# A mixture-of-experts decoder layer: moving the gather of each expert pair's rows, and the sums of the down biases, to other places in TensorE's order

## The chip, the core and the metric

The kernel runs on one core of a Trainium2 chip. The core has a matrix engine (TensorE, PE in the profile), a vector engine (VectorE, DVE), a scalar engine (ScalarE, ACT), GpSimd (POOL) and a queue that mostly issues transfers (SyncE, SP). The engines run side by side and wait for each other through semaphores. Each engine takes its own instructions in the order in which they are written. The metric is the device time of one execution in microseconds (us).

## The reference

The program computes one layer of a decoder for 288 tokens (256 of a prompt, 32 new ones of eight sequences): attention in two head groups, an output projection, a LayerNorm, and then a mixture of experts (MoE) with 32 experts, of which each token uses four. All numbers are float32. The change lies in the MoE, which is most of the time:

```python
def moe_ffn(hx, w_router, b_router, w_gate_up, b_gate_up, w_down, b_down):
    logits = jnp.matmul(hx, w_router).astype(jnp.float32) + b_router
    top_val, top_idx = lax.top_k(logits, TOP_K)                 # 4 of 32
    gates = jax.nn.softmax(top_val, axis=-1)
    comb = jnp.sum(jax.nn.one_hot(top_idx, N_EXPERTS) * gates[..., None], axis=1)

    def expert_step(acc, xs):
        wgu, bgu, wdn, bdn, c = xs                              # 1024x2048, 2048, 1024x1024, 1024
        gu = jnp.matmul(hx, wgu) + bgu
        gate = jnp.minimum(gu[:, 0::2], SWIGLU_LIMIT)
        up = jnp.clip(gu[:, 1::2], -SWIGLU_LIMIT, SWIGLU_LIMIT)
        act = gate * jax.nn.sigmoid(SWIGLU_ALPHA * gate) * (up + 1.0)
        y = jnp.matmul(act, wdn) + bdn
        return acc + c[:, None] * y.astype(jnp.float32), None
```

After it come a residual sum and a LayerNorm. The weights of the 32 experts are 403 MB, and every expert's weights are read once.

## The kernel before

The experts are taken in 16 pairs. A pair computes both experts side by side, each in one half (64 columns) of the matrix array, for at most 64 token rows ("slots") per expert. Further passes for experts with more rows are not taken in the profiled execution.

**Weights.** A pair's weights are 12 units of 2 MB: units 0 to 7 belong to the gate/up product, 8 to 11 to the down product. They go through a ring of 9 slots. SyncE issues each unit's transfer (`load_whole`, L508) as soon as its slot is free. For that it waits on counters that TensorE raises: `unit_used` after every second gate/up unit and after the second down unit, `gate_up_done` after unit 7, `down_done` after unit 11.

**One pair on TensorE** is, in this order:

- `begin_gate_up(i)` (L1267): the gate/up biases go into the four sum banks 0 to 3;
- `gate_up(i)` (L1171): units 0 to 7, each against a 128-row piece of the pair's turned rows `xg`. Behind unit 3 stands `combine(i - 1)` (L1251, L1237): the preceding pair's results are spread back to the tokens, five products that VectorE adds to `acc` (L2080);
- `gather(i + 1)` (L1051, L1055): the rows of the next pair are picked out of `hx` by products with a 0/1 matrix `pick`, into banks 6 and 7. ScalarE copies them to `xtok`, which is the same memory as `ybuf` (L1417);
- `turn_weights(i)` (L732 on `pickw`): the combining weights are transposed;
- `turn_act(i)` (L732 on `up`): the activations are transposed, in two halves of four; the first half waits for VectorE's products of the first two banks (`act_ready`), the second for those of the last two. ScalarE copies each half to `actT`;
- `down(i)` (L1224): units 8 to 11. Behind units 8 and 9 stand the transposes of the next pair's gathered rows (`turn_slots(i + 1)`, L732 on `ybuf`), which ScalarE scales into `xg` (L1562).

**VectorE** runs `swiglu(i)` when the four banks of gate/up are done: for each bank a minimum (L2062), a clip (L2063), a product (L2066), and, after ScalarE's sigmoid (L1571), the last product (L2071). It also makes the next `pick` matrix (`pick_slots`, L2046).

**The down biases** of all experts are summed once for all tokens, as products of the combining weights with the bias table (`add_biases`, L1122, and `add_sample_biases`, L1129). In the kernel before this stands between the down units of pair 12 (`finish_with_biases(MIDDLE, ...)`, with `MIDDLE = 12`).

`finish(i)` is the piece of TensorE's order that runs from the end of `gate_up(i)` to the end of `gate_up(i + 1)`. Nothing schedules these instructions: the order is the one written.

Of the kernel before, what the change touches and what calls it, by code (L numbers as in the profile page):

```python
# [26 lines left out]
PAIRS = E // 2  # L27
# [82 lines left out]
def build_layer(nc, x_prompt, x_sample, cache_k, cache_v, state_k, state_v, page_table, w_in, gn_moba,  # L110
# [222 lines left out]
    PERIOD = 3  # L333
# [3 lines left out]
    def slot_of(r, u):  # L337
        return (UNITS * r + u - 1) % RING
# [5 lines left out]
    def pass_slot(u):  # L344
        return u % 8

    def pass_value(i, u):

        if 4 <= u < 8:
            return i * 16 + (16 - 16 * PAIRS)  # L350
        return i * 32 + (16 * (u // 8 + 1) - 32 * PAIRS)
# [3 lines left out]
    def start_slot(u):  # L355

        return u if u < ASIDE else u - 1
# [5 lines left out]
    ln_bs = place("ln_bs", [128, 256], at=last_at + 9216)  # L363

    EARLY, WHOLE, LATE = range(3)
    MIDDLE = 12
    WHOLES = range(1, PAIRS - 1)
    USED_LATE = -2 * len(WHOLES)
    COPIES = 16 * (2 * DB + 5 + DB)
# [360 lines left out]
    def _(pe):  # L730
# [317 lines left out]
        def gather_samples():  # L1048
            for a in range(2):
                r = slice(NS * a, NS * a + NS)  # L1050
                nc.tensor.matmul(bank[6 + a][:, :], pick[r, 2, :], hx[r, 2, 512 * a:512 * a + 512], start=True, stop=False,  # L1051
                                 tile_position=(NS * a, 0))

        def gather_tile(t, a):
            return nc.tensor.matmul(bank[6 + a][:, :], pick[:, t, :], hx[:, t, 512 * a:512 * a + 512], start=False,  # L1055
                                    stop=(t == 1))
# [76 lines left out]
        def gather(i, turned_before):  # L1133
            pe.wait_ge(S.picked, i * 2 + 1)
            pe.wait_ge(S.actT_ready, turned_before)
            gather_samples()
            for a in range(2):
                gather_tile(0, a)
                gather_tile(1, a).then_inc(S.gathered, 1)
# [8 lines left out]
        def gate_up(i, m, odd, between={}, whole=False, further=False):  # L1148
            early = isinstance(i, int) and i == 0
            if not early:  # L1150
                begin_gate_up(i)
            for k in range(KC):
                w = [ring[slot_of(odd, k)][:, 2048 * e:2048 * e + 2048] for e in range(2)]
                if early:
                    pe.wait_ge(*((S.xg_ready, k // 4 + 1) if k % 4 == 3 else (S.first_slots, 3 * (k // 4) + k % 4 + 1)))
                if early:
                    w = [first[e] if k == ASIDE else ring[start_slot(k)][:, 2048 * e:2048 * e + 2048] for e in range(2)]
                    pe.wait_ge(*((S.first_in, 48) if k == ASIDE else (unit_in[start_slot(k)], 16)))
                elif further:
                    w = [ring[pass_slot(k)][:, 2048 * e:2048 * e + 2048] for e in range(2)]  # L1160
                    pe.wait_ge(half_in[pass_slot(k)], pass_value(i, k))
                elif whole:
                    w = [ring[slot_of(odd, k - k % 2 + e)][:, 2048 * (k % 2):2048 * (k % 2) + 2048] for e in range(2)]
                    if k % 2 == 0:
                        for u in (k, k + 1):
                            pe.wait_ge(unit_in[slot_of(odd, u)], unit_value(m, odd, u))
                else:
                    pe.wait_ge(unit_in[slot_of(odd, k)], unit_value(m, odd, k))
                for n in range(4):
                    for e in range(2):  # L1170
                        ins = nc.tensor.matmul(bank[n][64 * e:64 * e + 64, :], xg[:, k, 64 * e:64 * e + 64],  # L1171
                                               w[e][:, 512 * n:512 * n + 512], start=False, stop=(k == KC - 1))
                    if k == KC - 1:
                        ins.then_inc(S.gate_up_done, 1)
                if whole and k % 2 and k < KC - 1:
                    ins.then_inc(S.unit_used, 2)
                if not whole and k < KC - 1:
                    ins.then_inc(S.unit_used, 1)
                if k in between:
                    between[k]()  # L1180
# [61 lines left out]
        def combine(i):  # L1242
            pe.wait_ge(S.y_ready, i * 2 + 2)
            pe.wait_ge(S.spread_ready, i + 1)
            for j in range(5):
                t, half = divmod(j, 2)
                t0, rows = TILES[t]
                if j >= 2:
                    pe.wait_ge(S.added, i * 5 + (5 + j - 1))
                if t < 2:  # L1250
                    ins = nc.tensor.matmul(bank[4 + half][:, :], spread[:, t0:t0 + rows],  # L1251
                                           ybuf[:, 512 * half:512 * half + 512], start=True, stop=True)
                else:
                    ins = mix_samples(bank[4], True)
                ins.then_inc(S.mixed, 1)
# [14 lines left out]

        def finish(i, m, odd, m_next, whole=True, next_whole=True):

            gather(i + 1, i * 2)
            turn_weights(i, i * 2 + 3)
            turn_act(i, i * 2 + 4)
            down(i, m, odd, {0: lambda: turn_slots(i + 1, 0),
                             1: lambda: (pe.wait_ge(S.actT_ready, i * 2 + 2), turn_slots(i + 1, 1))}, whole)
            if m_next is not None:
                gate_up(i + 1, m_next, (odd + 1) % PERIOD, {3: lambda: combine(i)}, next_whole)

        def finish_with_biases(i, m, odd, m_next):

            def first_slots():
                turn_slots(i + 1, 0)
                turn_comb()

            def other_slots():
                pe.wait_ge(S.actT_ready, i * 2 + 2)
                turn_slots(i + 1, 1)
                for j in range(2):  # L1290
                    add_biases(j)

            def other_biases():
                for j in range(2, 4):
                    add_biases(j)
                add_sample_biases()

            gather(i + 1, i * 2)
            turn_weights(i, i * 2 + 3)
            turn_act(i, i * 2 + 4)  # L1300
            down(i, m, odd, {0: first_slots, 1: other_slots, 2: other_biases}, True)
            pe.wait_ge(S.bias_added, 5)
            gate_up(i + 1, m_next, (odd + 1) % PERIOD, {3: lambda: combine(i)}, True)

        begin_gate_up(0)
        logits_product(2)
# [3 lines left out]
        gate_up(0, 0, 0)  # L1310
        finish(0, 0, 0, 0, whole=False)
        finish(1, 0, 1, 0)
        finish(2, 0, 2, 1)

        def finish_three(m):
            finish(m * PERIOD, m, 0, m)
            finish(m * PERIOD + 1, m, 1, m)
            finish(m * PERIOD + 2, m, 2, m + 1)

        with pe.Fori(1, MIDDLE // PERIOD) as m:  # L1320
            finish_three(m)
        finish_with_biases(MIDDLE, MIDDLE // PERIOD, 0, MIDDLE // PERIOD)
        finish(MIDDLE + 1, MIDDLE // PERIOD, 1, MIDDLE // PERIOD)
        last = PAIRS - 1
        finish(last - 1, last // PERIOD - 1, 2, None)

        def keep_sums(t, half, stop=False):

# [83 lines left out]
    def _(act):  # L1412
# [138 lines left out]
        def take_gathered(i):  # L1551
            for a in range(2):
                act.wait_ge(S.gathered, i * 2 + (a + 1))
                copy(xtok[:, 512 * a:512 * a + 512], bank[6 + a][:, :]).then_inc(S.xtok_ready, 1)
# [13 lines left out]
        def sigmoids(i, ns=range(4)):  # L1568
            for n in ns:
                act.wait_ge(S.clipped, i * 4 + (n + 1))  # L1570
                nc.scalar.activation(sig[:, half_of(n)], gate[:, half_of(n)], ACT.Sigmoid, scale=SWISH).then_inc(S.sigmoided, 1)  # L1571
# [11 lines left out]
        def take_down(i):  # L1583
            act.wait_ge(S.down_done, i + 1)
            for half in range(2):
                copy(ybuf[:, 512 * half:512 * half + 512], bank[4 + half][:, :]).then_inc(S.y_ready, 1)

        take_gathered(0)
        take_slots(0)
        sigmoids(0)  # L1590

        def between_pairs(i):
            take_gathered(i + 1)
            take_weights(i)
            take_turned(i)
            take_slots(i + 1)
            take_down(i)

        def between_with_biases(i):
            take_gathered(i + 1)  # L1600
            take_weights(i)
            take_turned(i)
            act.wait_ge(S.comb_turned, 1)
            copy(combT[0:E, :], bank[3][0:E, 0:T]).then_inc(S.combT_ready, 1)
            take_slots(i + 1)
            take_down(i)

        with act.Fori(0, MIDDLE) as i:
            between_pairs(i)
            sigmoids(i + 1)  # L1610
        between_with_biases(MIDDLE)
        sigmoids(MIDDLE + 1)
        with act.Fori(MIDDLE + 1, PAIRS - 2) as i:
            between_pairs(i)
            sigmoids(i + 1)
        between_pairs(PAIRS - 2)
        sigmoids(PAIRS - 1, (0, 1))
        take_weights(PAIRS - 1)
        take_turned(PAIRS - 1, (0,))
# [607 lines left out]
```

## Time and profile before

| | us |
|---|---|
| median of 3 runs | 1141.97 |
| the 3 runs | 1142.9, 1140.39, 1141.97 |
| the profiled execution | 1139.37 |
| its span, first to last instruction | 1137.5 |
| PE busy in the span | 1099.5 |
| DVE busy | 293.1 |
| ACT busy | 203.6 |
| POOL busy | 30.0 |

The page divides the span into 40 slices of 28.4 us. The first 7 or so are the attention; the MoE fills the rest. The median lies 2.6 us above the profiled execution, 1.9 us of whose own time lie outside the span. In the views below, a time at a row's start is counted from the span's start; L with a number is a line of the kernel; `x16` is a count of instructions. A float32 product is two instructions in these records, so one unit is 16 of them.

### The profile page before, as it was taken

Reading aid. Unit: us, or ns where it says so; the run is one execution under the profiler, and the core shown is the slowest. Engines: PE = TensorE matmul, PEld = TensorE weight load, DVE = VectorE, ACT = ScalarE, POOL = GpSimd, SP = SyncE. Lnnn points to the kernel's source line nnn. Section 1 sums busy time; section 2 is a strip of 40 time slices with the busy share of each in tenths; the row PEclk is TensorE's granted clock in tenths of the full one; section 3 lists DMA queues with packets and bytes.
Section 4 is the critical chain, followed back from the end, with each engine's and each line's share of the span. In section 5 each row is a group of like instructions: output and inputs, shape, how many; then the busy total and the mean of one; then the engine's idle time right before and its main releaser. Section 6 shows DMA issues by size and latency. Waiting matters only on the chain.

```text
span 1137.5 us, 14116 instructions
## 1 busy us (share of the span) xinstructions
PE 1099.5 (97%) x5468; PEld 463.2 (41%) x5469; DVE 293.1 (26%) x734; ACT 203.6 (18%) x481; POOL 30.0 (3%) x65
## 2 busy tenths in 40 slices
PE   8999999999999999999999999999999999999996
PEld 6876764433333333333333333333333333333331
DVE  1553757530303030212121212120203031303033
ACT  2323412411111120202020202020201111111102
POOL 0110111000000000000000000000000000000001
PEclk9999999999999999999999999999999999999998
DMA  9967878999999999999999999999999999999994
GB/s 361 351 219 248 285 280 336 426 433 407 430 421 430 430 431 430 431 430 429 432 431 432 432 430 432 432 432 429 433 430 432 432 430 432 431 430 430 425 426 160
DMA packets 59172, 454.37 MB, mean 399 GB/s; under 512 B 6467, under 2 KB 19411, under 8 KB 31348
## 3 DMA queue, kind: packets, MB, share of 16 engines
q1 hardware_dynamic: 56642, 440.97, 92.7%
q0 software_dynamic: 1728, 10.75, 2.5%
q10 hardware_dynamic: 754, 1.98, 0.4%
q8 instruction: 34, 0.56, 0.2%
q14 instruction: 14, 0.11, 0.0%
HBM read 450.14 MB, written 11.93 MB: 406 GB/s over the span
## 4 chain that ended last, share of the span: by engine, by line
PE 83%; DMA 13%; ACT 2%; DVE 2%; issue 1%; SPq 0%; DVEq 0%
PE bank L1171 30%; PE bank L1224 19%; DMA ring<-in_w_gate_up 13%; PE bank L732 6%; PE bank L759 6%; PE bank L1055 5%; PE bank L1251 3%; PE bank L762 2%; PE bank L920 2%; PE bank L1051 1%; PE bank L1354 1%; PE bank L1267 1%; PE bank L877 1%; ACT ybuf L1417 1%; ACT actT L1417 1%; PE bank L851 1%
## 5 line engine op out<-in xcount | busy, mean ns | idle before, releaser
L1171 PE MATMUL bank<-ring,xg 128*64 128x512 f32 x2032 | 445.6, 594 | 10.8 <-DMA ring<-in_w_gate_up 10.8
L1171 PEld LDWEIGHTS bank<-ring,xg 128*64 128x64 f32 x2032 | 146.4, 137 | 299.3 <-issue 296.9
L1224 PE MATMUL bank<-ring,actT 128*64 128x512 f32 x960 | 216.2, 597 | 4.2 <-ACT actT L1417 4.2
L2080 DVE TENSOR_TENSOR acc<-acc,bank 128x512 f32<-128x512 f32 x60 | 41.3, 688 | 492.0 <-PE bank L1251 491.8
L1571 ACT ACTIVATE sig<-gate 128x256 f32<-128x256 f32 x64 | 26.5, 416 | 530.1 <-DVE gate L2062 530.1
L1224 PEld LDWEIGHTS bank<-ring,actT 128*64 128x64 f32 x960 | 67.3, 137 | 120.0 <-issue 115.3
L2062 DVE TENSOR_SCALAR gate<-bank 128x256 f32<-128x256 f32 x64 | 26.8, 419 | 186.8 <-PE bank L1171 186.8
L759 PE MATMUL bank<-xT,wblk 128*128 128x288 f32 x256 | 65.4, 409 | 0.3 <-DVE xT L1670 0.3
L1562 ACT ACTIVATE xg<-bank,small 128x128 f32<-128x128 f32 x128 | 48.0, 457 | 97.0 <-PE bank L732 96.9
L1055 PE MATMUL bank<-hx,pick 128*128 128x512 f32 x128 | 59.2, 605 | 0.0
L1417 ACT ACTIVATE ybuf<-bank 128x512 f32<-128x512 f32 x63 | 36.0, 596 | 126.7 <-PE bank L1224 87.4
L1251 PE MATMUL bank<-ybuf,spread 128*128 128x512 f32 x120 | 58.4, 619 | 0.0
L759 PEld LDWEIGHTS bank<-xT,wblk 128*128 128x128 f32 x256 | 47.5, 190 | 14.6 <-issue 2.7
L1055 PEld LDWEIGHTS bank<-hx,pick 128*128 128x128 f32 x128 | 23.0, 190 | 34.3 <-issue 34.3
L1251 PEld LDWEIGHTS bank<-ybuf,spread 128*128 128x128 f32 x120 | 19.2, 189 | 39.0 <-DVE acc L2080 19.7
L920 PE MATMUL bank<-wout,outT 128*128 128x512 f32 x64 | 29.8, 603 | 0.0
L762 PE MATMUL bank<-wblk,xT 128*128 128x256 f32 x128 | 29.0, 380 | 0.0
L2066 DVE SCALAR_TENSOR_TENSOR up<-up,gate 128x256 f32<-128x256 f32 x64 | 27.2, 425 | 3.3
L732 PEld LDWEIGHTS bank<-keep,ybuf 128*128 128x128 f32 x128 | 17.8, 207 | 25.3 <-issue 24.3
L723 POOL TENSOR_TENSOR acc<-acc,ln_b_sb 128x512 f32<-128x512 f32 x2 | 3.0, 1500 | 941.0 <-DVE acc L2186 941.0
L2063 DVE TENSOR_SCALAR up<-bank 128x256 f32<-128x256 f32 x64 | 26.5, 414 | 0.0
L2071 DVE TENSOR_TENSOR up<-up,sig 128x256 f32<-128x256 f32 x64 | 25.4, 419 | 0.0
(247 smaller groups left out, 672.3 us busy)
## 6 DMA issues: line engine op xcount, KB each, us to landing
ring<-in_w_gate_up SPq DMA_DIRECT2D x127, 2048.0 KB, 26.5
ring<-in_w_down SPq DMA_DIRECT2D x63, 2048.0 KB, 28.0
wblk<-in_w_in SPq DMA_DIRECT2D x11, 1024.0 KB, 8.7
kring<-in_cache_k_moba SPq DMA_DIRECT2D x16, 256.0 KB, 7.5
vring<-in_cache_v_moba SPq DMA_DIRECT2D x16, 256.0 KB, 7.2
out<-in_state_k_win POOLq DMA_DIRECT2D x8, 512.0 KB, 5.2
out<-in_state_v_win POOLq DMA_DIRECT2D x8, 512.0 KB, 6.1
kring<-in_state_k_win SPq DMA_DIRECT2D x16, 256.0 KB, 5.3
```

Source lines behind the costliest of these rows:

```text
L732: return nc.tensor.transpose(out, in_, ident[0:in_.shape[0], 0:in_.shape[0]])
L759: ins = nc.tensor.matmul(out[:, 0:T], w[:, k, 128 * c:128 * c + 128], xT[:, k, :], start=(k == 0), stop=(k == KC - 1))
L762: ins = nc.tensor.matmul(out[:, 0:256], xT[:, k, 128 * c:128 * c + 128], w[:, k, :], start=(k == 0), stop=(k == KC - 1))
L920: return nc.tensor.matmul(bank[2 * t + half][:, :], outT[:, k, t0:t0 + rows], wout[:, k, 512 * half:512 * half + 512], start=(k == 0), sto ...
L1055: return nc.tensor.matmul(bank[6 + a][:, :], pick[:, t, :], hx[:, t, 512 * a:512 * a + 512], start=False, stop=(t == 1))
L1171: ins = nc.tensor.matmul(bank[n][64 * e:64 * e + 64, :], xg[:, k, 64 * e:64 * e + 64], w[e][:, 512 * n:512 * n + 512], start=False, stop=( ...
L1224: ins = nc.tensor.matmul(bank[4 + half][64 * e:64 * e + 64, :], actT[:, j, 64 * e:64 * e + 64], w[e][:, at:at + 512], start=(j == 0), stop ...
L1251: ins = nc.tensor.matmul(bank[4 + half][:, :], spread[:, t0:t0 + rows], ybuf[:, 512 * half:512 * half + 512], start=True, stop=True)
L1417: return nc.scalar.activation(out, in_, ACT.Copy, **kw)
L1562: ins = nc.scalar.activation(xg[:, k, :], turned, ACT.Identity, bias=s_(c_cols + KC + k), scale=s_(c_cols + k))
L2066: V.scalar_tensor_tensor(up[:, c], up[:, c], 1.0, gate[:, half_of(n)], ALU.add, ALU.mult).then_inc(S.dve_moe, 1)
L2080: V.tensor_tensor(o, o, new, ALU.add).then_inc(S.added, 1)
```

## The change

`gather` of a pair's rows is issued from inside `gate_up` of the pair before, behind unit 5, so that for pair `i + 2` it stands in `gate_up(i + 1)` between units 5 and 6. It no longer stands between `gate_up` and `turn_weights`. Only the gather of pair 1 stays where it was. ScalarE's copies of the gathered rows (`take_gathered`) move in the same way: behind `take_down(i)` and ahead of the sigmoids. `MIDDLE` becomes 2, so that the down biases' sums stand in the third pair.

```diff
-    MIDDLE = 12
+    MIDDLE = 2
...
         def finish(i, m, odd, m_next, whole=True, next_whole=True):
 
-            gather(i + 1, i * 2)
+            if isinstance(i, int) and i == 0:
+                gather(1, 0)
             turn_weights(i, i * 2 + 3)
             turn_act(i, i * 2 + 4)
             down(i, m, odd, {0: lambda: turn_slots(i + 1, 0),
                              1: lambda: (pe.wait_ge(S.actT_ready, i * 2 + 2), turn_slots(i + 1, 1))}, whole)
             if m_next is not None:
-                gate_up(i + 1, m_next, (odd + 1) % PERIOD, {3: lambda: combine(i)}, next_whole)
+                gate_up(i + 1, m_next, (odd + 1) % PERIOD, {3: lambda: combine(i), 5: lambda: gather(i + 2, i * 2 + 2)}, next_whole)
...
-        finish(2, 0, 2, 1)
+        finish_with_biases(MIDDLE, 0, 2, 1)
...
-        def between_pairs(i):
-            take_gathered(i + 1)
+        take_gathered(1)
+
+        def between_pairs(i, gathers=True):
             take_weights(i)
             take_turned(i)
             take_slots(i + 1)
             take_down(i)
+            if gathers:
+                take_gathered(i + 2)
```

`finish_with_biases` changes in the same two lines as `finish`, and the loops are cut anew so that pair 2 is the one with biases.

TensorE's order in the program, at the end of the gate/up product of pair 1, before. `ring_85` and `ring_77` are the ring slots of the last two units (6 and 7):

```order
L1171 MATMUL bank<-ring_77,xg 64x512
L1051 MATMUL bank<-hx,pick 128x512 x2
L1055 MATMUL bank<-hx,pick 128x512 x4
L732 MATMUL bank<-keep,pickw 128x128 x2
L732 MATMUL bank<-keep,pickw 128x32
L732 MATMUL bank<-keep,up 128x128 x8
L1224 MATMUL bank<-ring_78,actT 64x512
```

The same place after the change, from the last product of unit 5 to the first of unit 6:

```order
L1171 MATMUL bank<-ring_83,xg 64x512
L1171 MATMUL bank<-ring_84,xg 64x512
L1051 MATMUL bank<-hx,pick 128x512 x2
L1055 MATMUL bank<-hx,pick 128x512 x4
L1171 MATMUL bank<-ring_85,xg 64x512
```

and from the last product of unit 7 into the down product:

```order
L1171 MATMUL bank<-ring_77,xg 64x512
L732 MATMUL bank<-keep,pickw 128x128 x2
L732 MATMUL bank<-keep,pickw 128x32
L732 MATMUL bank<-keep,up 128x128 x8
L1224 MATMUL bank<-ring_78,actT 64x512
```

The six gather products have moved ahead of the 16 products of units 6 and 7, and the transposes now stand directly behind unit 7.

ScalarE's order in the loop over pairs, after, from the down product's copies to the sigmoids (the two single `ybuf` rows are the gathered rows of the pair after next):

```order
L1562 ACTIVATE xg<-bank,small 128x128 x4
L1417 ACTIVATE ybuf<-bank 128x512 x2
L1553 ISA
L1417 ACTIVATE ybuf<-bank 128x512
L1553 REGISTER_ALU
L1417 ACTIVATE ybuf<-bank 128x512
L1570 ISA
L1571 ACTIVATE sig<-gate 128x256
```

In the kernel before the two single rows stand ahead of the copy to `spread`, behind the sigmoids.

## Rows read from the trace of the kernel before

**Rows 1.** The page: what the transfers moved in each of 40 slices.
```profile
GB/s 361 351 219 248 285 280 336 426 433 407 430 421 430 430 431 430 431 430 429 432 431 432 432 430 432 432 432 429 433 430 432 432 430 432 431 430 430 425 426 160
```
**Rows 2.** The chain that ended last, pair 1: start us, us, what.
```profile
268.74 1.07 PE bank L1267 x8
...
301.97 1.06 PE bank L1051 x4
303.02 3.65 PE bank L1055 x8
...
308.93 3.65 PE bank L1224 x16
312.59 0.67 PE bank L732 x4
```
**Rows 3.** The same chain, later pairs.
```profile
580.69 1.06 PE bank L1051 x4
...
587.50 3.65 PE bank L1224 x16
...
603.11 1.07 PE bank L1267 x8
...
659.02 28.31 DMA ring<-in_w_gate_up
...
892.29 28.44 DMA ring<-in_w_gate_up
...
1067.21 1.07 PE bank L1267 x8
```
**Rows 4.** Landing times of line L508's transfers issued in 225:320 and in 780:900.
```profile
DMA to landing us min/median/max: 9.0/13.2/17.8
...
DMA to landing us min/median/max: 26.5/31.5/35.8
```
**Rows 5.** Timeline behind pair 1's gate/up product: start us, us, engine, line.
```profile
303.16 0.42 DVE L2071 TENSOR_TENSOR up<-up,sig 128x256 f32<-128x256 f32 x1
...
303.94 0.42 ACT L1571 ACTIVATE sig<-gate 128x256 f32<-128x256 f32 x1 [1.04 <-DVE gate L2062]
...
304.62 0.75 DVE L2071 TENSOR_TENSOR up<-up,sig 128x256 f32<-128x256 f32 x2
...
308.19 1.09 ACT L1417 ACTIVATE actT<-bank 128x512 f32<-128x512 f32 x2 [0.60 <-PE bank L732]
```
**Rows 6.** Timeline, last pair: transposes that wait for VectorE; granted clock there.
```profile
1101.88 0.75 PE L732 MATMUL bank<-keep,up 128*128 128x128 f32 x4 [0.75 <-DVE up L2071]
...
1100.00:1105.00 5.00, 4.25 (x18) 1.88 (x16) 4.58 (x13) 1.92 (x5) 0.00 (x0) 1.00 1.02 429
```
**Rows 7.** The chain, down products of pair 12 (with biases) and pair 13.
```profile
934.91 3.65 PE bank L1224 x16
...
955.41 1.07 PE bank L1267 x8
...
995.66 3.65 PE bank L1224 x16
...
1011.26 1.07 PE bank L1267 x8
```
**Rows 8.** Timeline of VectorE, next `pick`; of TensorE, a wait in pair 7's unit 6.
```profile
622.86 0.55 DVE L2046 TENSOR_TENSOR pick<-keep,posm 128x384 f32<-128x384 f32 x1
...
629.03 0.42 PEld L1171 LDWEIGHTS bank<-ring,xg 128*64 128x64 f32 x4 [0.44 <-DMA ring<-in_w_gate_up]
```
**Rows 9.** The last units: their issue (SP), and TensorE's last down unit in the chain.
```profile
1082.71 11.69 SPq L523 DMA_DIRECT2D ring<-in_w_down  x2
...
DMA to landing us min/median/max: 31.2/31.2/31.2
...
1114.55 7.04 PE bank L1354 x32
```
**Rows 10.** A stretch: us, PE, PEld, DVE, ACT, POOL busy, clock, DMA share, GB/s.
```profile
260.00:270.00 10.00, 10.00 (x52) 3.42 (x50) 0.00 (x0) 2.59 (x6) 0.00 (x0) 1.00 0.98 388
```

More of the change, by code:

```diff
@@ L1296, in other_biases @@
                 add_sample_biases()
-            gather(i + 1, i * 2)
             turn_weights(i, i * 2 + 3)
@@ L1302, in finish_with_biases @@
             pe.wait_ge(S.bias_added, 5)
-            gate_up(i + 1, m_next, (odd + 1) % PERIOD, {3: lambda: combine(i)}, True)
+            gate_up(i + 1, m_next, (odd + 1) % PERIOD, {3: lambda: combine(i), 5: lambda: gather(i + 2, i * 2 + 2)}, True)
         begin_gate_up(0)
@@ L1318, in finish_three @@
             finish(m * PERIOD + 2, m, 2, m + 1)
-        with pe.Fori(1, MIDDLE // PERIOD) as m:
+        with pe.Fori(1, PAIRS // PERIOD - 1) as m:
             finish_three(m)
[L1322 to L1325, printed above, removed]
+        last, final = PAIRS - 1, PAIRS // PERIOD - 1
+        finish(last - 3, final, 0, final)
+        finish(last - 2, final, 1, final)
+        finish(last - 1, final, 2, None)
         def keep_sums(t, half, stop=False):
@@ L1597, in between_pairs @@
             take_down(i)
+            if gathers:
+                take_gathered(i + 2)
         def between_with_biases(i):
-            take_gathered(i + 1)
             take_weights(i)
@@ L1606, in between_with_biases @@
             take_down(i)
+            take_gathered(i + 2)
         with act.Fori(0, MIDDLE) as i:
@@ L1615, in _ @@
             sigmoids(i + 1)
-        between_pairs(PAIRS - 2)
+        between_pairs(PAIRS - 2, False)
         sigmoids(PAIRS - 1, (0, 1))
```

## The prediction

> **What bounds the kernel now.** I read the page first: PE is busy 1099.5 of 1137.5 us, 97% of the span, and the transfers run at 421 to 433 GB/s in every slice from the 11th to the 39th [rows 1]. Both look like the limit, so the page alone cannot say which one an edit on TensorE meets. The chain of waits can. In pair 1 it lies on TensorE alone: the pair begins at 268.74, the next one at 324.54 [rows 2], and up to the begin of pair 7 at 603.11 [rows 3] the mean is (603.11 - 268.74) / 6 = 55.73 us a pair. Then the chain changes: at 659.02 and four times more until 892.29 it holds a transfer of 28.3 to 28.5 us in each pair [rows 3]. These pieces come every (892.29 - 659.02) / 4 = 58.32 us, which is what a pair's 25.2 MB take at 431 GB/s.
>
> So there are two clocks. TensorE needs 55.73 us a pair, the weights 58.32. TensorE starts late, behind the attention, while the ring has long been full; it then gains 2.59 us a pair on the transfers until it has caught up at about pair 8: 7 x 2.59 = 18.1 us of lag at the begin of pair 1. The time from issue to landing tells the same from the other side. The longer TensorE lags, the later slots are freed and the shorter the line of transfers ahead of a new one: its median is 13.2 us in the first stretch and 31.5 in the late pairs [rows 4], 18 us more. The first small wait of TensorE for a unit stands at 629.03 [rows 8].
>
> At the end the two are level again. The biases in pair 12 cost TensorE time that it wins back in two pairs, and pair 15 begins at 1067.21 [rows 3], where the transfers' pace alone would put it at 892.1 + 3 x 58.32 = 1067.1. What counts for the end is therefore whether TensorE still lags when pair 15 begins.
>
> **The gather inside gate/up.** The six gather products are 12 instructions, 1.06 + 3.65 = 4.71 us from 301.97 [rows 2]. They are neither added nor removed; only what runs beside them changes. In 14 pairs (1 to 14) they now stand between units 5 and 6, where TensorE has other work anyway, so there they cost their full 4.71 us. What is won is behind unit 7. Before, the gate/up product ends at G = 301.97, where the gather begins, and the down product starts at 308.93 [rows 2]: 6.96 us, of which 4.71 are gather. In pair 6 it is 587.50 - 580.69 = 6.81 [rows 3]; I take the middle, 6.89.
>
> After the change this stretch has another bound, since the gather covered VectorE's work. VectorE ends the product of the second bank at 303.16 + 0.42 = G + 1.61 and that of the fourth at 304.62 + 0.75 = G + 3.40 [rows 5]. None of that hangs on the gather: VectorE starts from the gate/up banks, and ScalarE's sigmoids were ahead of the gather's copies too. TensorE can turn the weights at once, then waits until G + 1.65 for the first half of the activations, turns them, and waits until G + 3.44 for the second half. That half stands ahead of the down product in TensorE's order, so nothing of the down product can start before it. A wait of this kind is in the last pair of before, 0.75 us for VectorE [rows 6]. Four transposes take 0.67 us [rows 2], so down starts at G + 4.11 to 4.2; I take 4.15. ScalarE is not later: its last sigmoid ends at 303.94 + 0.42 = G + 2.39, then come the copy to `spread` and the first half of `actT` (1.09 us for both halves), which end near G + 3.4 [rows 5]. The second half's copy lies beside the first down unit.
>
> Bounds: down cannot start before G + 3.40 + 0.67 = 4.07. If it had to wait for the second half's copy too, as it now waits for the first, it would be 3.44 + 0.75 [rows 6] + 0.6 + 0.1 = 4.9. I stay near the lower one, because down's first unit asks only for the first half.
>
> Per pair: + 4.71 (gather in its new place) + 4.15 - 6.89 = + 1.97 us. TensorE's period becomes 55.73 + 1.97 = 57.70 us. What goes is the small wait for ScalarE's copy of the gathered rows; what is late in its stead is VectorE's last product.
>
> In its new place the gather waits for nothing. Its matrix `pick` is written at 622.86 to 623.41, and unit 6 begins at about 629.0 [rows 8]: 5.6 us to spare. ScalarE's two copies fall between the down copies and the sigmoids, where ScalarE is idle, and the 6.9 us of units 6 and 7 cover them. Units 6 and 7 free their slots 4.7 us later against the pair's begin. SyncE's order is the same, and behind these two issues stand those of later units; nobody needs them as long as TensorE lags, and this too only matters for a TensorE that waits for weights.
>
> **The biases.** From the first down unit to the next pair's begin it is 955.41 - 934.91 = 20.50 us with biases and 1011.26 - 995.66 = 15.60 without [rows 7]: 4.90 us. They cost that in pair 2 as in pair 12. Before, they stood where TensorE had 2.6 us a pair to spare behind them; now they are added to the lag at its largest.
>
> **The sum.** Pair 15 begins at 268.74 + 14 x 57.70 + 4.90 = 1081.4 by TensorE's own pace. By the lag: 18.1 + 4.9 - 14 x (58.32 - 57.70) = 14.3 us behind the transfers' 1067.1, the same time. TensorE would win back only 0.62 us a pair, so it lags all the way to the end and the chain never goes over to the transfers. From the begin of pair 15 on both kernels have the same instructions, and before TensorE does not wait for a unit there. So the whole 1081.4 - 1067.2 = 14.2 us reach the end: 1139.37 + 14.2 = 1153.6 us for an execution like the profiled one. The median of before lies 2.6 us above its profiled execution. Most of a kernel paced by TensorE does not see differences in the transfers, so I carry about a third of this over: 1154.5 us.
>
> Own range: 0.3 us more or less a pair is 4 us, thus 1150 to 1159; with 4.9 us behind every gate/up product (0.75 more in 14 pairs) it would be 1165.
>
> **Rival 1: the transfers hide it (no change).** The kernel moves weights at 430 GB/s from pair to pair, and a TensorE period of 57.70 is still under 58.32. If the lag of the first pairs did not persist, or TensorE's new period were shorter by 1 us, pair 15 would begin when its weights let it and the time would stay at 1142. For it speaks the chain from 659 to 892. Against it: for no lag at pair 15, TensorE's period would have to be under 58.32 - (18.1 + 4.9) / 14 = 56.68 us, 1.0 less than I forecast, so down would have to start at G + 3.1, ahead of VectorE's last product. The Trainium skill (Perfetto Trace Analysis, section Roofline) bounds a core by its 16 DMA engines at about 435 GB/s. By that rule this kernel is at its ceiling, with 430 to 432 in most slices of this trace, and work moved about on TensorE is worth nothing; that would be this rival. The rule tells the rate, and not that TensorE starts 18 us behind.
>
> **Rival 2: faster.** Early in the MoE the transfers dip to 388 GB/s for 10 us [rows 10], since slots are freed in bursts, and the tenth slice, 256 to 284, has 407 against 430 [rows 1]: 28.4 x 23 / 430 = 1.5 us. At the end the last unit lands at about 1082.7 + 31.2 = 1113.9, and TensorE takes it at 1114.55 [rows 9], 0.65 us later. If the gather behind unit 5 spread the releases so that these dips close, if down's earlier start made up for the gather, and if the biases off the tail removed the last 0.65 us, the kernel would be paced by the transfers throughout and end 1.5 + 0.65 = 2.2 us earlier, at 1139.8, about 0.2%. It decides from the same point as rival 1 (a TensorE period under about 56.7), and asks for more.
>
> **Rival 3: the clock.** TensorE now idles twice about 1 us behind each gate/up product, with only transposes between. Before it idled so for 0.75 us in the last pair, at a granted clock of 1.00, that is 2.4 GHz [rows 6]. If the grant fell to 1.2 GHz there, one down unit of 3.65 us taking twice that in 14 pairs would be 51 us more: 1205. Nothing in the rows speaks for it. The Trainium skill (TensorE: Matmul & The Clock Gate, Part 4) says that transposes do not count as busy for the clock in the way other products do; here the clock was 1.00 through the stretches with transposes, so the trace does not show it.
>
> **Chances.** Forecast 0.86, rival 1 0.08, rival 2 0.03, rival 3 0.03. The forecast's own spread leaves about 0.06 outside 1147 to 1161, so with the rivals 0.2 lie outside. A difference under 0.2% (2.3 us) could not be told from none: faster 0.03, same 0.08, slower 0.89.
>
> **What would show it.** In the profile after, the pairs begin every 57.7 us from pair 1 to pair 15 (62.6 once, from pair 2 to 3), and pair 15 begins near 1081. The first `up` transposes wait for VectorE (L2071) in pairs 1 to 14, about 1 us for each half, and down starts 4.1 to 4.2 us behind gate/up. The chain holds no transfer of weights. The time to landing stays short, nowhere near 31 us in the late pairs, since the line of transfers grows by no more than 0.62 us a pair. Wrong would be: a chain with transfers in late pairs (rival 1), a wait in front of the gather, or a period over 58.3, with DMA slices under 430.

## The result and the profile after

| | before | after |
|---|---|---|
| median of 4 runs, us | 1142.2 | 1168.99 |
| the runs, us | 1140.39 to 1142.9 | 1166.64 to 1169.8 |
| the profiled execution, us | 1139.37 | 1169.06 |
| its span, us | 1137.5 | 1167.3 |

The change makes the kernel slower: ratio 1.0234, 95% interval 1.0215 to 1.0253, or 26.8 us between the medians. The direction and the mechanism of the forecast hold; the size does not. 1154.5 was forecast, in a range of 1147 to 1161, and the difference is twice the forecast one.

The first thing to see is in the page's slices of the profile after, what the transfers moved. In [rows 1] they stood near 430 from the 13th slice on; now single slices in the middle are lower:

```profile
GB/s 359 331 216 245 276 293 340 426 424 415 425 398 431 400 431 384 430 430 430 430 431 419 432 416 432 428 432 431 431 431 431 422 431 413 431 426 429 426 325 42
```

The chain of waits of the profile after, from the begin of pair 1 to the begin of pair 2 (start us, us, what; VectorE's pieces before the last are left out). It answers to [rows 2]:

```profile
271.69 1.07 PE bank L1267 x8
...
298.06 1.06 PE bank L1051 x4
299.11 3.63 PE bank L1055 x8
302.74 4.47 PE bank L1171 x20
...
312.75 0.43 DVE up L2073
...
313.22 0.75 PE bank L732 x4
313.97 3.58 PE bank L1224 x16
...
329.51 1.07 PE bank L1267 x8
```

The gather stands inside gate/up at its full 4.69 us. Behind gate/up, which ends at G = 309.69, VectorE's last product is now in the chain, and down begins at 313.97 = G + 4.28, where 4.15 was forecast. The pair takes 329.51 - 271.69 = 57.82 us (57.70 forecast). The table of who waited for whom, TensorE, after, shows what took the place of the wait for ScalarE's copy:

```profile
PE bank L732 <- DVE up L2073: 31.7, 29, 1.5
```

That is 29 waits of 1.1 us in the mean, two in each of 14 pairs and one (0.75 us) in the last. No wait of TensorE for a weight transfer is in this table any more; before, its products had ten, two in each of the pairs 8 to 12 (the wait of [rows 8] is one of a weight load). The transfers' time to landing, issued in 780 to 900, stays at a median of 15.0 us, where it was 31.5 [rows 4]:

```profile
DMA to landing us min/median/max: 9.7/15.0/20.5
```

So far the profile is what was forecast. The rest is in pairs 3, 6, 7, 11 and 12. The chain after, pair 6, from the second half of the activations' transposes to the next pair:

```profile
609.34 1.12 PE bank L732 x4
610.46 6.07 PE bank L1224 x16
616.53 0.68 PE bank L732 x4
617.21 3.58 PE bank L1224 x16
...
628.49 1.07 PE bank L1267 x8
```

Down's first unit takes 6.07 us, and 3.58 us in other pairs; the four transposes take 1.12 us, and otherwise 0.75. The stretches over these rows (us, busy PE, PEld, DVE, ACT, POOL, granted clock, DMA share, GB/s) give the reason: over the slow unit the mean granted clock is 0.58, near half of the 2.4 GHz, and around it 1.00.

```profile
545.00:552.00 7.00, 4.83 (x25) 2.17 (x21) 6.29 (x17) 2.47 (x6) 0.00 (x0) 1.00 1.02 438
603.00:610.00 7.00, 4.75 (x24) 2.28 (x21) 6.29 (x17) 2.46 (x6) 0.00 (x0) 0.90 1.01 433
610.00:616.50 6.50, 6.50 (x20) 1.72 (x18) 0.00 (x0) 0.60 (x1) 0.00 (x0) 0.58 1.02 436
723.00:730.00 7.00, 4.83 (x25) 2.17 (x21) 6.29 (x17) 2.46 (x6) 0.00 (x0) 1.00 1.01 431
904.00:910.00 6.00, 6.00 (x16) 1.55 (x16) 0.00 (x0) 0.60 (x1) 0.00 (x0) 0.59 1.00 429
```

In the first and the fourth of these rows (pairs 5 and 8) TensorE waited just as long behind gate/up, and the clock held. Here is the whole difference of the two profiled executions, 1169.06 - 1139.37 = 29.7 us, by the begins of the pairs:

| term | how | us |
|---|---|---|
| before pair 1 | 271.69 - 268.74 | 2.95 |
| 14 pairs at the full clock | 14 x 57.82 + 4.90, less 1067.21 - 268.74 | 15.9 |
| slow down products | the five periods over 57.82: 2.1, 2.9, 1.5, 2.9, 1.5 | 11.0 |
| from pair 15 on | (1167.3 - 1097.0) - (1137.5 - 1067.2) | 0.0 |

Of the third term 0.5 us are not the clock's. The period of pair 3, the one behind the biases, is 58.28 and not 57.82 also where the clock holds (e3 below); in after, the first wait for VectorE is 1.48 us there and 1.1 to 1.2 elsewhere. That leaves 10.5 us for the clock.

The first term is not the change's: code and order are the same up to there. TensorE's first 32 input products take 10.34 us instead of 8.00, and that comes and goes between executions. The chain of before and that of after:

```profile
9.30 8.00 PE bank L759 x32
...
9.91 10.34 PE bank L759 x32
```

In the trace of after these products start every 0.48 us until 14.7 us and every 0.24 us from there on; in that of before they start every 0.24 us from 9.6 us on. Half the pace is what 1.2 in place of 2.4 GHz would give. The first record of the clock in each trace fits: it grants the full clock from 8.1 us on before and from 14.7 on after. (The views show 1.00 ahead of the first record too.) In the profiles of the experiments pair 1 begins at 268.87 and 269.13 in the two where these products take 8.0 us (first record at 8.7 and 8.0 us), and between 270.66 and 271.55 in the nine others (13.1 to 14.6 us). The profiled execution of before has an early start, which is most likely why it lay 2.6 us under its median; no slower execution of it was profiled.

### The profile page after: what moved, and what is told of

It reads as the page before. It is cut to its first block, busy times and chain, and to the rows that moved or that the text cites. A ratio compares the mean times of both kernels' runs of the same rounds, so it can differ in the third digit from the quotient of the medians.

```text
span 1167.3 us, 14176 instructions
## 1 busy us (share of the span) xinstructions
PE 1117.6 (96%) x5468; PEld 460.6 (39%) x5469; DVE 292.2 (25%) x734; ACT 203.9 (17%) x481; POOL 30.1 (3%) x65
## 4 chain that ended last, share of the span: by engine, by line
PE 90%; DVE 6%; issue 2%; ACT 1%; DMA 0%; DVEq 0%
PE bank L1171 35%; PE bank L1224 19%; PE bank L732 6%; PE bank L759 6%; PE bank L1055 5%; PE bank L1251 5%; PE bank L762 2%; PE bank L920 2%; DVE gate L2064 2%; DVE up L2073 2%; PE bank L1267 1%; PE bank L1051 1%; DVE up L2065 1%; PE bank L1354 1%; PE bank L877 1%
## 5 line engine op out<-in xcount | busy, mean ns | idle before, releaser
L1171 PEld LDWEIGHTS bank<-ring,xg 128*64 128x64 f32 x2032 | 141.8, 137 | 292.2 <-issue 292.0
L1224 PE MATMUL bank<-ring,actT 128*64 128x512 f32 x960 | 224.8, 617 | 0.3 <-ACT actT L1417 0.3
L2064 DVE TENSOR_SCALAR gate<-bank 128x256 f32<-128x256 f32 x64 | 26.8, 419 | 248.6 <-PE bank L1171 248.6
L732 PE MATMUL bank<-keep,up 128*128 128x128 f32 x128 | 25.4, 327 | 32.1 <-DVE up L2073 31.7
L732 PEld LDWEIGHTS bank<-keep,up 128*128 128x128 f32 x128 | 18.5, 211 | 38.0 <-DVE up L2073 20.9
## 6 DMA issues: line engine op xcount, KB each, us to landing
ring<-in_w_down SPq DMA_DIRECT2D x63, 2048.0 KB, 15.6
```

The lines of the kernel that those rows point to most:

```text
L732: return nc.tensor.transpose(out, in_, ident[0:in_.shape[0], 0:in_.shape[0]])
L1224: ins = nc.tensor.matmul(bank[4 + half][64 * e:64 * e + 64, :], actT[:, j, 64 * e:64 * e + 64], w[e][:, at:at + 512], start=(j == 0), stop ...
L2064: V.tensor_scalar(gate[:, half_of(n)], bank[n][:, 0:512:2], LIMIT, None, ALU.min).then_inc(S.clipped, 1)
```

## The experiments

Each was timed in rounds with the kernel before on the same chip; ratios are to it in these rounds, with 95% intervals, so that they are not quotients with the 1142.2 above. "Period" is the usual time between the begins of two pairs where the clock holds, and the last column tells in how many pairs a down product met a fall of the clock; both are read from each profile.

| kernel | median us | ratio | period us | slow down products |
|---|---|---|---|---|
| e1 biases alone | 1142.34 | 1.0009 (0.9998 to 1.0019) | 55.7 | none |
| e2 gather alone | 1167.63 | 1.0231 (1.0208 to 1.0255) | 57.82 | in 5 pairs |
| e3 both waits filled with products | 1158.02 | 1.0150 (1.0130 to 1.0170) | 57.81 | none |
| e4 both filled with transposes | 1165.41 | 1.0220 (1.0198 to 1.0242) | 57.81 | in 1 pair, see below |
| e5 gather split | 1146.59 | 1.0039 (1.0023 to 1.0055) | 57.13 | none |
| e6 small gather | 1140.83 | 0.9990 (0.9978 to 1.0001) | 54.48 | in 5 pairs |
| e7 first wait filled | 1158.05 | 1.0140 (1.0120 to 1.0160) | 57.82 | none |
| e8 second wait filled | 1157.88 | 1.0141 (1.0122 to 1.0160) | 57.82 | none |
| e9 split, samples together | 1143.15 | 1.0009 (1.0000 to 1.0019) | 56.45 | none |
| e10 no clip | 1144.96 | 1.0018 (1.0006 to 1.0030) | 56.75 | in 2 pairs |
| e11 small gather, waits filled | 1140.86 | 0.9988 (0.9978 to 0.9998) | 54.48 | none |

**The two parts apart: e1 and e2.** e1 is the kernel before with one edit in effect:

```diff
-    MIDDLE = 12
+    MIDDLE = 2
```

> Kernel before with one part of the change alone: the down biases' sums stand in pair 2 instead of pair 12; the gather stays behind gate/up. Theory (cover and lag): TensorE's period stays 55.7 us, so the 4.9 us of the biases make the lag 23 us at pair 3, and it is won back at 2.6 us a pair by pair 10 or 11; the end is paced by the transfers and the time is that of before or up to 0.65 us less, 1141 to 1142. Rival (the biases are what costs): they come at the largest lag and nothing gives them back, 1142 + 4.9 = 1147.

Measured 1142.34 us, no difference. The chain of e1 goes over to the transfers one pair later than in [rows 3]; its first piece with a transfer in the MoE, and the next:

```profile
722.52 27.27 DMA ring<-in_w_gate_up
779.60 28.54 DMA ring<-in_w_gate_up
```

The biases are won back. e2 is the kernel after with `MIDDLE = 12`.

> Kernel after with the biases put back into pair 12; the gather stays between units 5 and 6. Theory (cover and lag): TensorE lags to the end wherever the biases stand, so the time is that of after, 1167 to 1169, and the period between pairs is 57.8 us where the clock holds. Rival (the biases' place is a part of the loss): 1169 - 4.9 = 1164 or less.

Measured 1167.63 us, within 1.4 us of the kernel after. The gather is the whole loss. Its slow down products are in pairs 6, 7, 11, 12 and 13, four of them pairs that are slow in the profile after too. What picks these pairs no run shows.

**The idle time and the clock: e3, e4, e7, e8.** The kernel after, with work in the waits (pairs 1 to 14):

```diff
+        def fill():
+            nc.tensor.matmul(bank[5][:, :], ident, hx[:, 0, 0:512], start=True, stop=True)
...
             turn_weights(i, i * 2 + 3)
-            turn_act(i, i * 2 + 4)
+            pe.wait_ge(S.added, i * 5 + 5)
+            fill()
+            turn_act(i, i * 2 + 4, (0,))
+            fill()
+            turn_act(i, i * 2 + 4, (1,))
```

> Kernel after, with one useless product (128x512, into bank 5, which the down product overwrites) ahead of each half of the activations' transposes in pairs 1 to 14, where TensorE only waits (1.1 and 1.0 us; a product takes 0.9). Theory (the idle time behind gate/up lets the clock fall): the granted clock stays 1.00 at every down product, pairs come every 57.8 us, and the 11 us of slow down products in the profile after are gone: 1156 to 1158. Rival (the clock falls whatever stands there, as in some executions anyhow): slow first down units as in after, 1167 to 1170.

Measured 1158.02 us (four runs within 0.5 us): 11.0 less than after, and the period is unchanged. By the begins of the pairs, from pair 1 to pair 15, it is 814.9 us in e3 and 825.3 in after: the 10.5 us of above. The granted clock over the span rose from 0.987 to 0.997. In e3's chain pair 1 is that of after to 0.01 us:

```profile
270.87 1.07 PE bank L1267 x8
...
312.39 0.75 PE bank L732 x4
313.14 3.58 PE bank L1224 x16
...
328.68 1.07 PE bank L1267 x8
```

TensorE did more work and the kernel became faster. So the clock fell because of what is missing in the waits behind gate/up, and not in some executions anyhow. e4 asks whether transposes do as well:

```diff
         def fill():
-            nc.tensor.matmul(bank[5][:, :], ident, hx[:, 0, 0:512], start=True, stop=True)
+            for n in range(5):
+                turn(bank[5][:, 128 * (n % 4):128 * (n % 4) + 128], hx[:, 0, 128 * n:128 * n + 128])
```

> The same as the kernel with useless products, but the idle time is filled with five useless transposes (128x128, 0.85 us) in each of the two waits. Theory A (any work of TensorE holds the clock): 1156 to 1158 and no slow down product. Theory B (transposes do not count for the clock as other products do): the clock falls as in after or oftener, 1167 to 1180.

Measured 1165.41 us, between the two, and for a reason that neither theory had. Of its 14 periods 12 are like e3's (57.81, and 58.29 once, as e3 has 58.28). The two others are 62.82 and 61.56. There TensorE stood still for a cause that the trace names only "issue", as the timeline of TensorE in e4 shows at pair 6 (start us, us, line, in brackets the idle time before):

```profile
603.46 0.61 PE L732 MATMUL bank<-keep,pickw 128*128 128x128 f32 x3 [1.84 <-issue]
...
608.95 0.58 PE L732 MATMUL bank<-keep,up 128*128 128x128 f32 x2 [2.92 <-issue]
609.46 4.96 PE L1224 MATMUL bank<-ring,actT 128*64 128x512 f32 x16
```

Four such pauses make 8.2 us in e4, two in pair 6 and two in pair 9; after has none behind gate/up. What causes them was not tried, but the DMA view bears on it. e4 loads instructions in the middle of the loop over pairs, 19 times of 16 KB in 590:950:

```profile
q8 instruction: 19, 0.31, 0.3%
```

The same view of after and of e3 has no such load. One load ends inside each pause (at 601.8 and 607.6 in pair 6, at 780.4 and 786.4 in pair 9); the 15 others stand beside none. e4's loop has more instructions than e3's, so the pauses are probably waits for code. A slow down unit (4.96 us) follows the pauses of pair 6, and in pair 9 the clock falls over the transposes. In the 12 pairs without a pause the transposes held the clock, as the products did, though TensorE still waited 0.4 to 0.8 us twice in each. So e4 is for its theory A, in those pairs, and its total is no measure of it.

e7 leaves out the second `fill()`, e8 the first.

> Kernel with useless products, but only in the first wait, ahead of the first half of the activations' transposes; the second wait of 1.0 us stays idle. If the idle time in sum decides, the clock falls rarer than in after or no more: 1158 to 1163. If each wait of 1 us is enough by itself: as after less at most a third, 1164 to 1168.

> The same with the useless product only in the second wait; the first wait of 1.1 us stays idle. Idle time in sum decides: 1158 to 1163, like the kernel that fills the first. One of the two waits decides: this or the other kernel is at 1158, its twin at 1165 or more.

Both are at e3's time (1158.05 and 1157.88), and all their runs have a clock of 0.996 or 0.997. Neither wait alone decides; with about half of the idle time left, 1.0 us in e7 and 1.2 in e8, the clock held in every pair. (e10 below is not so clean.)

**Was it cover? e5, e9, e10.** e5 splits the gather:

```diff
-                gather(1, 0)
+                gather(1, 0)
+            else:
+                gather(i + 1, i * 2, (1,))
...
-{3: lambda: combine(i), 5: lambda: gather(i + 2, i * 2 + 2)}
+{3: lambda: combine(i), 5: lambda: gather(i + 2, i * 2 + 2, (0,))}
```

> Kernel after with the gather split: the products for bank 6 stand between units 5 and 6, those for bank 7 behind unit 7, ahead of the weights' transposes (2.36 us each). Theory (the gather was cover for VectorE's work): half of it covers enough, since TensorE needs only 3.5 us until the last product of VectorE and the transposes and the copy of bank 7 end at 4.55 us behind unit 7; the period is 55.7 + 2.36 + 4.55 - 6.89 = 55.75 us, nearly that of before, the lag is won back, no clock falls, and the time is 1141 to 1143. Rival (products between units 5 and 6 cost by standing there, in proportion): half of the loss without clock, 1142 + 8 = 1150.

Measured 1146.59 us, between the two expectations, so as it stands it tells neither. Its chain shows why the period is 57.13 and not 55.75:

```profile
297.91 1.05 PE bank L1051 x2
298.96 1.92 PE bank L1055 x4
300.87 7.02 PE bank L1171 x32
307.89 1.05 PE bank L1051 x2
308.94 1.93 PE bank L1055 x4
...
313.13 1.04 PE bank L1224 x3
```

Two instructions on the 32 sample rows take the 1.05 us that four take in [rows 2] (1.06): the products for the two banks, on different sets of 32 rows, run side by side there, and one after the other once they are torn apart. In sum the products take 5.95 us in e5 and 4.71 in [rows 2]: 1.05 us more for the torn pair and 0.2 for the others, and that is nearly all of the 1.4 us by which the period is longer than expected. e9 keeps them together:

```diff
-            gather_samples(halves)
+            if 0 in halves:
+                gather_samples()
```

> The split gather again, but the two products of the sample rows (32 rows, banks 6 and 7), which ran side by side when they stood together, stand together between units 5 and 6; behind unit 7 are only the two tile products of bank 7. Theory (cover): gate/up is 1.06 + 1.82 = 2.88 us longer, the down product starts at 4.28 us behind unit 7 as in after, bounded by VectorE's last product, so the period is 55.73 + 2.88 + 4.28 - 6.89 = 56.0 us, the lag is won back by pair 11 and the time is 1141 to 1143. Rival (placement between units 5 and 6 costs in proportion to what stands there): 2.88 of 4.71 us, 61% of 15.8 us: 1152.

Measured 1143.15 us, ratio 1.0009, against 1152 by the rival. With 63% of the gather in the new place at most 0.2% is lost, so the place as such costs nothing that shows in the time; what costs is to take away more cover than VectorE leaves to spare. In the profile TensorE waits for weights again from pair 12 on, as it did before from pair 8. In pair 14, behind such a wait of 2.63 us, the clock falls inside gate/up, and that pair takes 61.3 us; what this has to do with the 1.2 us between the medians is open. The period is 56.45 and not 56.0, since ScalarE's copy of bank 7 starts only behind its last sigmoid and the transposes wait for that copy. Here is pair 5, where gate/up ends at 536.15:

```profile
538.19 0.42 ACT L1575 ACTIVATE sig<-gate 128x256 f32<-128x256 f32 x1 [1.04 <-DVE gate L2070]
...
538.52 0.60 ACT L1421 ACTIVATE ybuf<-bank 128x512 f32<-128x512 f32 x1
...
539.17 1.25 PE L732 MATMUL bank<-keep,up 128*128 128x128 f32 x8 [0.65 <-ACT ybuf L1421]
...
540.70 3.65 PE L1225 MATMUL bank<-ring,actT 128*64 128x512 f32 x16 [0.28 <-ACT actT L1421]
```

So down starts at G + 4.55, where 4.28 was expected.

e10 takes the other side, with less work on VectorE. It leaves out the clip of the up values:

```diff
-                    V.tensor_scalar(up[:, c], bank[n][:, 1:512:2], LIMIT, -LIMIT, ALU.min, ALU.max).then_inc(S.dve_moe, 1)
                     dve.wait_ge(S.clipped, i * 4 + (n + 1))
-                    dve.wait_ge(S.dve_moe, i * 8 + (2 * n + 1))
-                    V.scalar_tensor_tensor(up[:, c], up[:, c], 1.0, gate[:, half_of(n)], ALU.add, ALU.mult).then_inc(S.dve_moe, 1)
+                    V.scalar_tensor_tensor(up[:, c], bank[n][:, 1:512:2], 1.0, gate[:, half_of(n)], ALU.add, ALU.mult).then_inc(S.dve_moe, 2)
```

> Kernel after with less work on VectorE behind gate/up: the clip of the up values (L2065) is left out and the next product reads the bank, so that a bank takes about 1.1 instead of 1.45 us. Theory (VectorE's last product sets the start of down, and the idle time lets the clock fall): last product about 2.3 us behind unit 7 instead of 3.5, down at about 3.1 instead of 4.28, period 56.6 us, lag nearly won back at pair 15, idle time about 1 us and no fall of the clock: 1142 to 1146. Rival (down's start hangs on something else, as ScalarE's copies or the transposes' own issue): period 57.8 as before and 1158 to 1168.

Measured 1144.96 us. The timeline of e10 in pair 1, where gate/up ends at 309.07:

```profile
310.73 0.75 DVE L2071 TENSOR_TENSOR up<-up,sig 128x256 f32<-128x256 f32 x2
...
311.53 0.75 PE L732 MATMUL bank<-keep,up 128*128 128x128 f32 x4 [0.78 <-DVE up L2071]
...
312.21 2.37 PE L1224 MATMUL bank<-ring,actT 128*64 128x512 f32 x10
```

VectorE's last product ends at G + 2.4 and down starts at G + 3.1, as expected. That the clock would not fall was expected too, and that missed: in pairs 9 and 13 it falls, and down's first unit takes 5.33 us. TensorE waits 0.3 to 0.5 and 0.7 to 0.8 us in each pair, in sum as long as in e7 and e8, where no pair fell. So the idle time in sum is not all that decides; what else does is open. The whole kernel is 24 us faster by taking 64 small instructions from an engine that is busy a quarter of the time.

**The lag: e6 and e11.** e6 is the kernel after with a gather of 32 columns a bank in place of 512 (the other columns are not computed), e11 the same with both waits filled as in e3:

```diff
+            small = not (isinstance(i, int) and i == 1)
+            gather_samples(32 if small else 512)
             for a in range(2):
-                gather_tile(0, a)
-                gather_tile(1, a).then_inc(S.gathered, 1)
+                gather_tile(0, a, 32 if small else 512)
+                gather_tile(1, a, 32 if small else 512).then_inc(S.gathered, 1)
```

> Kernel after, where the gather of pairs 2 to 15 computes only the first 32 of each bank's 512 columns (the other columns of the gathered rows are not computed), at the same places. Theory (lag): the six products cost their full 4.7 us there; with them nearly gone the period falls to about 57.8 - 4.3 = 53.5 us, TensorE catches up by pair 6, and the transfers pace the end: 1141 to 1143. The idle time behind unit 7 is the same, so the clock still falls in some pairs; where TensorE has time to spare that costs nothing. Rival (something else than TensorE's pace holds the kernel, as later releases of the ring's slots or the waits behind unit 7 alone): little is gained, 1155 to 1165.

Measured 1140.83 us. The table of TensorE's waits in e6 has both rows now, VectorE and the transfers:

```profile
PE bank L732 <- DVE up L2074: 31.8, 29, 1.5
PE bank L1172 <- DMA ring<-in_w_gate_up: 15.7, 11, 2.7
```

The same 32 us of waits for VectorE, and a clock of 0.979 to 0.990, cost nothing here, because TensorE is ahead of the transfers. The period is 54.48, a full us above the 53.5 expected: what is left of the six products takes 1.35 us (0.34 + 1.01), and I had taken 0.4.

> The kernel with the small gather (only the first 32 columns of each bank's gathered rows are computed for pairs 2 to 15) and the two useless products per pair in the waits behind unit 7. Theory: the falls of the clock in the small-gather kernel (granted clock 0.98 to 0.99 over the span) lie in pairs where TensorE waits for weights anyway, so that they cost nothing there; without them the clock is 0.997 and the time the same within 0.1%, 1140 to 1142. Rival (a slow down product costs also where the transfers pace the kernel): 3 to 10 us less than the small-gather kernel's 1140.8.

Measured 1140.86 us, the same as e6 to 0.03 us (by the ratios 0.9988 and 0.9990). The five slow down products of e6 are gone. The clock did not go to 0.997 as expected but to 0.991 to 0.995: four falls are left in the profile, inside gate/up, in pairs where TensorE waits up to 2.7 us for weights. The rival, 3 to 10 us of gain, is out. Together the two say also what is to be gained at all by a lighter TensorE in this stretch: 1.1 to 1.4 us, about 0.1%. No version tried that computes everything beats the kernel before.

## Why the prediction was wrong

- **Two clocks, and a TensorE that starts behind.** Right. e1, e6 and e9 are the same as before within 0.1%, with periods of 55.7, 54.48 and 56.45, and the kernels at 57.8 are not. The rule used in the sum, loss = 18.1 + 4.9 - 14 x (58.32 - period), gives for the period of e3 15.9 us, for e10 1.0 and with its two slow units of 1.7 us 4.4, for e5 6.3, and for e9 less than nothing. Read at the begin of pair 15, less the later begin of pair 1, the profiles have 16.4 us in e3, 4.6 in e10 and 6.3 in e5, so there the rule is good to 0.5 us. The medians of e10, e5 and e9 lie 3.0, 4.4 and 1.2 us above that of the kernel before. In e1 the stretch from 380 to 400 moves 402 GB/s and before 431: with the largest lag slots come free so late that the transfers run short, which probably shifts their pace a little, and the rule has no term for it.
- **The gather costs its full 4.71 us in its new place.** Right: 4.69 us.
- **Down at 4.15 us behind gate/up.** A term too small by 0.13: the transposes' second half starts at G + 3.53, not 3.44, and takes 0.75 us, not 0.67. The period is 57.82 and not 57.70; in 14 pairs that is 1.7 us of the 15.9.
- **The biases.** Right, 4.9 us of TensorE's time in pair 2; the 0.5 us more in pair 3 was not foreseen. In e1 they are won back; in e2, without them at pair 2, nothing is gained.
- **"So the whole 14.2 us reach the end" and the clock.** This is the step that failed. The sum was made at a granted clock of 1.00 throughout. The clock was in the text as rival 3, with the right place and the right mechanism ("if the grant fell to 1.2 GHz there"), but with a chance of 0.03, on "Nothing in the rows speaks for it", and at the price of a fall in all 14 pairs. It fell in 5 of 14, for 10.5 us in the profile; e3, without the falls, is 11.0 us under after and inside the forecast's range. Forecast and rival were treated as either-or, while a part of the rival belonged into the sum's range: 0 to 51 us, with the forecast below it.
- **The third of the 2.6 us.** The profiled execution of before has TensorE's first products done about 2 us sooner than most profiles, and a kernel that TensorE paces keeps that to its end. All of the 2.6 us should have been carried over, not 0.9: 1.7 us. With the clock (10.5 to 11.0), the period (1.7) and pair 3 (0.5) that makes the 14.5 us between 1154.5 and 1168.99.
- **What the rows could have told.** The one idle wait of this kind before was 0.75 us, once [rows 6]. The change brings two of 1.1 us in each pair, three times as much in one place, and no row of before shows a clock after that. A row with less of the cause is no evidence against the effect. The Trainium skill (TensorE: Matmul & The Clock Gate, Part 4) warned at this place that transposes do not keep the clock up as other products do. The fall it made me price did come, but not for that reason as far as e4 shows: in 12 pairs five transposes in each wait held the clock. By e4 what lacked was work, and not products in place of transposes.
- **Rivals 1 and 2** did not come: the chain after has no transfer of weights, and pair 15 begins at 1097.0, 15.6 us behind the forecast 1081.4: the start (2.95), the clock (10.5), the period (1.7) and pair 3 (0.5).

## What to carry to other kernels

Before moving work out of a gap, ask what the gap was hiding: here it covered 3.5 us of another engine's work, and the work moved cost its full time elsewhere and left the wait behind. Compare periods, not busy shares, to see which of two paces rules, and carry the lag at the start along: a stage that is faster than its transfers can still be late for all its life. And where a change makes TensorE idle in each round, put the clock into the sum and its range; if it falls, a useless product in the wait can be the cheapest remedy.

## What the runs showed of the hardware

- A down unit of 16 instructions takes 3.58 us at a granted clock of 1.00 and up to 6.07 us where the grant fell to half. With two waits of 1.1 us per pair, transposes between, the grant fell in 5 of 14 pairs in the profiles of after and e2, in four of them in the same pairs; with one of the two waits filled (e7, e8) in none; with waits of 0.4 and 0.7 us (e10) in two. Transposes in the waits held it in all 12 pairs without a pause (e4).
- When the transfers pace the kernel, slow down products cost nothing (five in e6, none in e11; 1140.83 and 1140.86 us).
- Four instructions on 32 rows each, two of them on another set of rows, take 1.06 us together; two alone take 1.05 us (e5).
- The first 32 input products take 8.0 us in some executions and 9.9 to 10.4 in others of the same code. In the late ones TensorE works at half the pace until 13.1 to 14.7 us, when the first record of the full granted clock stands; pair 1 begins 1.5 to 3.0 us later.
- Four pauses of TensorE of 1.3 to 2.9 us (e4) stand beside loads of instructions, which no other profile has in the middle of its loop.
